# Attention of a two-layer hybrid decoder trunk: eleven score batches instead of fourteen, and their values in fewer stretches

## What is computed

```python
# branch A (dsa): 8 heads, one shared key and value, top-64 keys by an index score
s = einsum('bqhd,bqkd->bhqk', qb, kg); p = masked_softmax(s, sel <= t); out = einsum('bhqk,bqkd->bqhd', p, vg)
# branch C (nsa): 8 heads, two key groups; cmp: 15 compressed blocks, sel: chosen blocks, win: window of 256
o = gb[..., 0:1] * o_c + gb[..., 1:2] * o_s + gb[..., 2:3] * o_w
# merge: three sigmoid gates of 1024 columns each, then the output projection
merged = g_a * (y_a @ proj_a) + g_b * (y_b @ proj_b) + g_c * (y_c @ proj_c);  x = x + merged @ w_out
```

## Time and profile before

| | |
|---|---|
| median of three runs | 1203.36 us |
| the profiled execution's own time | 1202.76 us |
| its span (first to last instruction) | 1201.0 us |
| PE busy | 1178.2 us, 98% |
| DVE busy | 980.3 us, 82% |
| ACT busy | 617.2 us, 51% |
| mean granted PE clock | 0.997 |

### The profile page before, as it was taken

The page is one execution under the profiler, slowest core; times in us unless marked ns, Lnnn a source line. Parts: engine busy times, 40 slices in busy tenths (PEclk is TensorE's granted clock), DMA queues, the critical chain, the costliest instruction groups (busy, mean ns, idle before and its releaser), DMA issues.

```text
span 1201.0 us, 18918 instructions
## 1 busy us (share of the span) xinstructions
PE 1178.2 (98%) x6442; PEld 965.9 (80%) x6442; DVE 980.3 (82%) x2128; ACT 617.2 (51%) x1038; POOL 71.8 (6%) x151
## 2 busy tenths in 40 slices
PE   7999999999999999999999999999999999999996
PEld 5888888887777888888888888888877788888885
DVE  6988886668979698888798888775798796989886
ACT  6444446646664464444464444465566645444442
POOL 5300000420000000000000000024000000000000
PEclk9999999999999999999999999999999999999998
DMA  9654554552445455455565555545444354555553
GB/s 352 248 177 179 204 187 163 190 187 97 159 152 185 173 195 201 179 208 179 206 228 196 205 183 201 210 146 188 132 150 141 141 211 154 210 209 178 207 202 130
DMA packets 37288, 223.53 MB, mean 186 GB/s; under 512 B 6769, under 2 KB 9457, under 8 KB 11377
## 3 DMA queue, kind: packets, MB, share of 16 engines
q1 hardware_dynamic: 35792, 217.14, 50.7%
q10 hardware_dynamic: 1408, 5.65, 1.4%
q0 software_dynamic: 32, 0.00, 0.0%
HBM read 218.58 MB, written 1.05 MB: 183 GB/s over the span
## 4 chain that ended last, share of the span: by engine, by line
PE 87%; DVE 8%; issue 2%; ACT 1%; ACTq 0%; DVEq 0%
PE G L1332 21%; PE G L1334 21%; PE G L1333 21%; DVE wlo L916 3%; PE TO L1334 3%; PE TO L1332 3%; PE TO L1333 3%; PE SC L1332 3%; PE SC L1334 3%; PE SC L1333 3%; PE SC L1515 1%; PE TO L1562 1%; DVE sm L1128 1%; DVE probs L1155 1%; PE TO L1348 1%
## 5 line engine op out<-in xcount | busy, mean ns | idle before, releaser
L916 DVE TENSOR_TENSOR wlo<-raw,whi 128x1024 fp32r<-128x1024 f32 x398 | 471.4, 1226 | 107.6 <-ACT whi L572 105.8
L572 ACT ACTIVATE whi<-raw 128x1024 fp32r<-128x1024 f32 x398 | 399.0, 1052 | 256.0 <-PE G L1334 137.2
L1332 PE MATMUL G<-whi,xhi 128*128 128x512 f32 x1184 | 464.1, 392 | 8.2 <-DVE wlo L916 4.8
L1333 PE MATMUL G<-wlo,xhi 128*128 128x512 f32 x1184 | 457.6, 386 | 0.0
L1334 PE MATMUL G<-whi,xlo 128*128 128x512 f32 x1184 | 457.5, 386 | 0.0
L1332 PEld LDWEIGHTS G<-whi,xhi 128*128 128x128 f32 x1184 | 222.3, 188 | 61.2 <-DVE wlo L916 7.0
L1334 PEld LDWEIGHTS G<-whi,xlo 128*128 128x128 f32 x1184 | 222.4, 188 | 46.0
L1333 PEld LDWEIGHTS G<-wlo,xhi 128*128 128x128 f32 x1184 | 222.6, 188 | 42.8
L1005 DVE STREAM_TRANSPOSE shared_q<-shared_q 32x128 f32<-32x128 f32 x640 | 193.6, 303 | 8.3
L641 ACT ACTIVATE shared_q<-G,stat 128x256 f32<-128x256 f32 x88 | 41.9, 476 | 79.0 <-PE G L1334 74.5
L744 ACT ACTIVATE probs<-sm,stat 128x128 f32<-128x128 f32 (+1 forms) x96 | 42.6, 445 | 57.6 <-DVE stat L1134 57.6
(11 more groups left out here) (180 smaller groups left out, 965.6 us busy)
## 6 DMA issues: line engine op xcount, KB each, us to landing
raw<-stream SPq DMA_DIRECT2D x200, 1024.0 KB, 4.8
gates<-w_in ACTq DMA_DIRECT2D x2, 2048.0 KB, 8.4
z<-z SPq DMA_DIRECT2D x32, 64.0 KB, 4.5
x<-x_in SPq DMA_DIRECT2D x4, 256.0 KB, 6.0
raw<-stream SPq DMA_DIRECT2D x2, 512.0 KB, 5.7
out<-x SPq DMA_DIRECT2D x4, 256.0 KB, 2.0
small<-small_in ACTq DMA_DIRECT2D x2, 414.5 KB, 3.3
const<-const_in SPq DMA_DIRECT2D x1, 690.0 KB, 12.2
```

The source lines that it names most:

```text
L572: act.activation(whi[s][:, c], raw[s][:, c], ACT.Copy).then_inc(hi_done, 1)
L916: dve.tensor_tensor(wlo[s][:, c], raw[s][:, c], whi[s][:, c].bitcast(F32), ALU.subtract).then_inc(lo_done, 1)
L1332: pe.matmul(o, ahi, bhi, start=first, stop=False)
L1333: pe.matmul(o, ahi, blo, start=False, stop=False)
```

## The change

`BATCHES` gets eleven entries. The two halves of sel, win and dsa for `qt` 0 become one batch of eight heads (8 x 128 columns); cmp of `qt` 0 is now batch 2. The values come at four steps of the gate stage, several groups one behind the other, and none is left for the projection stage; dsa of `qt` 1 sums into other columns of the PSUM banks (`col`), so it needs no wait for the copy of dsa `qt` 0. Copies, `selection_bias` and `topk_round` move to other steps. The code ahead of the gate stage is not touched, but its batches 0 and 1 are now sel and win of `qt` 0 with eight heads each.

```diff
-BATCHES = _nsa(0) + _nsa(1) + [("dsa", qt, g) for qt in range(2) for g in range(2)]
+BATCHES = [
+    ("sel", 0, 0), ("win", 0, 0), ("cmp", 0, 0),
+    ("sel", 1, 0), ("sel", 1, 1), ("win", 1, 0), ("win", 1, 1), ("cmp", 1, 0),
+    ("dsa", 0, 0), ("dsa", 1, 0), ("dsa", 1, 1)]
-VALUE_GROUPS = [(0, 1), (2, 3), (4,), (5, 6), (7, 8), (9,), (10, 11), (12, 13)]
-VALUES_AT = {1: 0, 3: 1, 4: 2, 6: 3, 8: 4, 9: 5, 11: 6}
+VALUE_GROUPS = [(0,), (1,), (2,), (3, 4), (5, 6), (7,), (8,), (9, 10)]
+VALUES_AT = {2: (0, 1, 2), 4: (3,), 7: (4, 5), 10: (6, 7)}
-SLOT_FREE = {5: 1, 7: 2, 10: 4, 12: 5}
+SLOT = {0: 0, 1: 1, 3: 2, 4: 3, 5: 0, 6: 1, 8: 2, 9: 0, 10: 1}
+SLOT_FREE = {5: 1, 6: 2, 8: 4, 9: 5}
...
 def heads_of(b):
-    return 8 if BATCHES[b][0] == "cmp" else 4
+    kind, qt, _ = BATCHES[b]
+    return 4 if kind != "cmp" and qt else 8
...
 # ACT, gate stage
-                    if k in (5, 10):
-                        split_o("nsa", k // 10, ychi, 0)
+                    if k in (3, 8):
+                        split_o("nsa", k // 8, ychi, 0)
...
                 split_o("dsa", 0, xhi, 4)
+                split_o("dsa", 1, xhi, 4)
                 split(l, at, 26)
                 split(l, at, 27)
-                split_o("dsa", 1, xhi, 4)
...
 # DVE, gate stage and after
-                    weigh(k + 1)
-                    if k in (5, 10):
-                        split_o(3 + k // 10, k // 10, ychi, yclo, 0)
-                    if k == 8:
+                    if k + 1 < NB:
+                        weigh(k + 1)
+                    if k in (3, 8):
+                        split_o(3 + k // 8, k // 8, ychi, yclo, 0)
+                    if k == 6:
                         selection_bias()
...
-                    if k < 4:
+                    if k in (0, 1, 2, 5):
                         topk_round()
                 gated(0, 1, 0, 0)
-                split_o(5, 0, xhi, xlo, 4)
                 gated(0, 1, 0, 1)
-                weigh(13)
+                split_o(6, 0, xhi, xlo, 4)
+                split_o(6, 1, xhi, xlo, 4, P)
...
-                split_o(6, 1, xhi, xlo, 4)
+                gated(1, 2, 1, 0)
                 split(l, at, 28)
-                gated(1, 2, 1, 0)
...
 # PE
-                    pairs = range(4) if kind == "cmp" else range(2 * g, 2 * g + 2)
+                    pairs = range(4) if heads_of(b) == 8 else range(2 * g, 2 * g + 2)
...
-                    if opens.get(n):
-                        pe.wait_ge(o_drained, l * 4 + opens[n])
+                    if n in (3, 6):
+                        pe.wait_ge(o_drained, l * 4 + n // 3)
+                    col = P if n == 7 else 0
...
-                    if k in VALUES_AT:
-                        strip_values(VALUES_AT[k])
+                    for n in VALUES_AT.get(k, ()):
+                        strip_values(n)
...
                 project(0, 1, ybhi, yblo, 0)
-                strip_values(7)
```

More of the change, by code:

```diff
@@ L83 @@
 KC = K_BAND + len(WINDOWS) * BANDC
-def _nsa(qt):
-    return [("sel", qt, 0), ("sel", qt, 1), ("win", qt, 0), ("win", qt, 1), ("cmp", qt, 0)]
-BATCHES = _nsa(0) + _nsa(1) + [("dsa", qt, g) for qt in range(2) for g in range(2)]
+BATCHES = [
+    ("sel", 0, 0), ("win", 0, 0), ("cmp", 0, 0),
+    ("sel", 1, 0), ("sel", 1, 1), ("win", 1, 0), ("win", 1, 1), ("cmp", 1, 0),
+    ("dsa", 0, 0), ("dsa", 1, 0), ("dsa", 1, 1)]
 NB = len(BATCHES)
@@ L122 @@
 PER_BANK = [sum(b == k for b in TURN_BANK.values()) for k in range(4)]
[L125 to L129, removed]
 def trunk(nc, x_in, pos_in, stream, small_in, w1_in, const_in, final_in, out):
@@ L362, in after, with strip_sums @@
             return (l + 1, 0) if occ else (l, 1)
-        strip_sums = TO[:, :, 0:P].rearrange("p a (k i) -> p a k i", k=4)
+        def strip_sums(col):
+            return TO[:, :, col : col + P].rearrange("p a (k i) -> p a k i", k=4)
         def by_strips(dst, ks, tok):
@@ L735, in exps @@
                     else:
-                        w, p = n, probs[:, slot_of(b), :]
+                        w, p = n, probs[:, SLOT[b], :]
                     if b >= 2:
@@ L764, in split_o @@
                     act.wait_ge(values_done, l * NG + GROUP_END[branch, tok])
-                    act.activation(by_strips(dst, ks, tok), strip_sums, ACT.Copy).then_inc(t_hi_done, 1)
+                    col = P if (branch, tok) == ("dsa", 1) else 0
+                    act.activation(by_strips(dst, ks, tok), strip_sums(col), ACT.Copy).then_inc(t_hi_done, 1)
                 for f in range(3):
@@ L1151, in weigh @@
                             then(dve.tensor_tensor(f, f, gate, ALU.mult))
-                    own = cmp_probs if kind == "cmp" else probs[:, slot_of(b), :]
+                    own = cmp_probs if kind == "cmp" else probs[:, SLOT[b], :]
                     turned = cmp_probsT if kind == "cmp" else own
@@ L1156, in weigh, with split_o @@
                     dve.transpose(turned[:, 0 : nh * w], own[:, 0 : nh * w]).then_inc(turned_probs, 1)
-                def split_o(n_hi, tok, dst_hi, dst_lo, ks):
+                def split_o(n_hi, tok, dst_hi, dst_lo, ks, col=0):
                     dve.wait_ge(t_hi_done, l * 10 + n_hi)
                     dve.tensor_tensor(
-                        by_strips(dst_lo, ks, tok), strip_sums, by_strips(dst_hi, ks, tok).bitcast(F32), ALU.subtract
+                        by_strips(dst_lo, ks, tok), strip_sums(col), by_strips(dst_hi, ks, tok).bitcast(F32), ALU.subtract
                     ).then_inc(o_drained, 1)
@@ L1542, in strip_values @@
                         pe.wait_ge(dsa_v_in, (l + 1) * 16 * 16)
-                    opens = {0: 0, 3: 1, 6: 2, 7: 3}
-                    if opens.get(n):
-                        pe.wait_ge(o_drained, l * 4 + opens[n])
+                    opens = (0, 3, 6, 7)
+                    if n in (3, 6):
+                        pe.wait_ge(o_drained, l * 4 + n // 3)
+                    col = P if n == 7 else 0
                     for kk in range(1 if kind == "cmp" else 4 * (qt + 1)):
@@ L1558, in strip_values @@
                                     }[kind]
-                                    slot, w = slot_of(group[0]), P * (qt + 1)
-                                    p = probs[rows, slot : slot + 2, 0 : 4 * w].rearrange(
-                                        "p g (h e k) -> p g h e k", h=2, e=2)[:, :, :, grp, STRIP * kk : STRIP * (kk + 1)]
+                                    slot, keys = SLOT[group[0]], slice(STRIP * kk, STRIP * (kk + 1))
+                                    if qt:
+                                        p = probs[rows, slot : slot + 2, :].rearrange(
+                                            "p g (h e k) -> p g h e k", h=2, e=2)[:, :, :, grp, keys]
+                                    else:
+                                        p = probs[rows, slot, :].rearrange("p (h e k) -> p h e k", h=4, e=2)[:, :, grp, keys]
                                 ins = pe.matmul(
-                                    TO[grp * HD : (grp + 1) * HD, a, 0:P], v, p, start=n in opens and kk == 0, stop=True,
-                                    skip_group_check=True)
+                                    TO[grp * HD : (grp + 1) * HD, a, col : col + P], v, p, start=n in opens and kk == 0,
+                                    stop=True, skip_group_check=True)
                     ins.then_inc(values_done, 1)
```

## The result

The changed kernel takes 1217.66 us, the median of six runs (1213.97 to 1220.19); the kernel before, beside it, 1202.78 (1202.61 to 1203.86). The ratio is 1.0117, with a 95% interval from 1.0099 to 1.0135: **14.9 us slower**, where the prediction had 1211.7 and a range to 1216.5. The direction holds; the size is above the range. The runs of after also scatter by 6 us, those of before by 1.3.

What follows compares the result with a forecast made beforehand. TensorE, busy for 98% of the span, bounds the kernel. Per layer 8.45 us of new waits less 2.6 less 1.7 gives + 4.15; two layers, + 8.3 on 1202.76, and 0.6 for the median give 1211.7, range 1205.0 to 1216.5.

Steps and rivals of the forecast that it cites:

- The bound: Whole kernel: TensorE busy for 98% of the span, so the time is its work plus its few waits.
- the chain of lateness: Ahead of the gate stage: eight-head exps and weighs delay each other, exps(1) starting at 276.56 and `yblo` 5.9 us late.
- The three large waits: TensorE, gate stage: 2.3 us before the scores of batch 3, 3.65 in mid chunk 2, 2.0 in mid chunk 4.
- The waits that go: TensorE's waits in chunk 6 (1.6 us) and the projection stage (about 1.0) vanish, together 2.6 per layer.
- the sum: Per layer 8.45 us of new waits, less 2.6 of waits gone, less 1.7 of seams: + 4.15, forecast 1211.7.
- rival D: Gate stage: TensorE's clock halves in a 3.65 us wait, the next chunk takes 5.4 more; 1222.5 us, chance 0.04.
- next to nothing: TensorE at the start of chunk 2: the wait for the `wlo` of unit 13, whose first half is done at 287.1.
- a join: Values directly behind values on TensorE: four seams per layer go, 0.1 us each taken, 0.4 in all.
- The 0.5 of chunk 10: TensorE waits 0.5 us at chunk 10, as step 8's copy of O and following work take 10.2 against 9.5.
- B: Lateness ahead of step 1 is absorbed, only small gains and losses stay: 1.8 us a layer faster, 1199.8; chance 0.08.
- C: First waits come, later ones (2.0 and 0.5) don't, since VectorE is ahead: 1.65 us a layer, 1206.7; chance 0.12.
- the round trip of step 3: From batch 4's scores to half of unit 16: VectorE needs 11.8 us, TensorE does 9.7, so a 2.0 wait.

## Why the prediction was wrong

**What held.** The bound, and the chain of lateness through exps(0), exps(1), `ybhi` and `yblo`, to a tenth of a microsecond. The three large waits within a quarter. That the order around batches 0 and 1 is the cause: two moves there give back 13.7 us. The waits that go: chunk 6 has none. And the sum: the kernel with its waits filled, which is the kernel after without the half clock, measures 1212.0, where I forecast 1211.7; that it agrees so closely is in part luck, since smaller errors cancel (below).

**What failed is the step on rival D**, "in a wait of 3.65 TensorE's granted clock falls and the next chunk runs at 1.2 GHz". I gave it 0.04 and left its cost out of the sum and of the range. The evidence against it was one wait of 1.5 us in chunk 6 with nothing behind it; from that I argued to waits of 2.3 and 3.65, longer than any that the trace had inside the work, where that row says nothing. The longest there is one that the prediction does not name, in the first SwiGLU, also with nothing behind it (TensorE's timeline, before):

```profile
24.09 0.50 PE L1332 MATMUL G<-whi,xhi 128*128 128x512 f32 x1 [1.78 <-DVE shared_q L994]
```

Against my 0.04 stood the measured end of the kernel, where idleness does lower the clock. The chance should have been above one half. All thirteen traces together, waits of TensorE behind the first 13 us, by their rows:

| wait | how many | half clock in it or behind it |
|---|---|---|
| 3.2 to 3.4 us | 7 | 6 |
| 1.9 to 2.3 us | 14 | 9 |
| 1.6 to 1.8 us (all in the first SwiGLU) | 13 | 2 |
| 1.1 to 1.5 us | 12 | 0 |

All 17 stretches of half clock that the windows view has ahead of TensorE's last work are in this table, each from within such a wait or up to 1.8 us behind its end. These are counts of one traced execution of each kernel, not a law.

**Its price was also wrong, the other way.** I took 5.4 us, a whole chunk at half clock. A stretch lasted 3.4 us in 14 of the 17 cases and cost 1.5 where TensorE had work; where the next wait followed at once it cost nothing. The other three lasted 6.8 us; one cost some 2.7 (layer 1 of the kernel with only the wait of chunk 2 empty is 7.5 slower than before, that of the filled kernel 4.8). But there were four in the profile, not two: three that cost. For the profiled execution that closes, with the waits and seams taken from the filled kernel: 1202.76, + 0.6 at the start, + 4.56 + 4.77, + 3 x 1.5 of clock = 1217.2, against 1217.34. The other runs have mean clocks from 0.987 to 0.993, and the order of their times is that of their clocks (1220.19 at 0.987; 1213.97 and 1214.85 at 0.993). That the number of such stretches changes from run to run and makes the scatter is read from this and from the filled kernel, which scatters by 0.9; the runs themselves were not traced.

The Trainium skill (TensorE: Matmul & The Clock Gate, "HAM oscillation") describes a kernel whose tiles start cold after each wait for operands. The runs here agree that a wait does it, inside a kernel whose TensorE is busy for 97%; they differ in that 6 of the 21 waits of 1.9 to 3.4 us were not followed by it.

**Smaller terms**, layer 0, that nearly cancel:
- The start of chunk 2 waits 0.36 (1.43 less 1.07 by starts), where I had "next to nothing". Chunk 2's wait is shorter for it, 3.40 instead of 3.65.
- Several groups of values in a row save more than 0.1 a join. The first three take 2.15 together (297.22 to 299.37); apart, 1.06, 1.06 and 0.40 before, 2.52 in all. The four joins save 0.8 instead of 0.4, about the whole 0.19 of an interruption each.
- The projection stage keeps half of its wait: 0.5 instead of nothing. Chunk 8 has a wait of a quarter of a microsecond that I did not foresee; chunk 10 has 0.3 (0.5).
- An eight-head score stretch takes 1.09, not 1.06.
- The 0.5 of chunk 10 was a slip: its own terms, 10.2 against 9.5, give 0.7. It measured 0.3.

Put together for layer 0: 8.6 of waits, less 2.1 of waits that went, less 2.0 of seams is 4.5, where the forecast had 8.45, 2.6 and 1.7.

Forecast 4.15 a layer, without the clock measured 4.56 and 4.77.

**The rivals.** B and C are out: `yblo` is 5.9 late, and the wait in chunk 4 is there. C's argument, that VectorE would have caught up, fails as it was put: the round trip of step 3 starts at the scores. That this round trip is what makes the wait in chunk 4 is shown by taking the top-k round and the copy out of it: 2.1 falls to 0.25.

**Left open.** Why one wait was followed by half clock and another of the same length was not: in the kernel after, the 3.4 of layer 0 was not, and the 2.25 before the scores of batch 3 was in layer 1 and not in layer 0. The runs give counts for it and no rule.

## What to carry to other kernels

When batches are merged, walk the order of the other engines again: a wider piece in front of a piece that the next engine wants costs its whole extra width there, and merging paid only after two pieces changed places (1217.7 to 1204.0) and two small jobs moved out of tight round trips (to 1196.9). A wait of 2 us or more on a TensorE that was busy until then is to be priced at its own length and a chance of half clock behind it (here 15 of the 21 waits of 1.9 us or more by their rows), some 1.5 us each time, and the range has to reach that far. Here its mark was scatter between runs of one kernel, with a mean clock that goes along. If such a wait can't be removed, unread multiplications in it keep the clock, here for 5.6 us.

## What the runs showed that I had not expected

- The granted clock fell to one half inside the work behind waits of 2.1 us in a kernel at a mean clock of 0.991, for 3.4 us, and in two other kernels behind a wait of 1.8 us by its row in the first SwiGLU, which all thirteen traces have (1.6 to 1.8).
- Filling a wait with multiplications whose result nobody reads was worth 5.6 us, and narrows six runs' 6.2 us of scatter to 0.9 in five.
- A half-clock stretch that ended in another wait was free (7.68 against 7.67 us).
- Small multiplications (32 x 64) of different groups behind each other saved the interruption's 0.19 us nearly in full (0.37 for the first two joins).
